# Summing gathered expert rows on TensorE four at a time instead of two, with eleven steps of the second stream placed earlier

## What is computed

```
def _peer(h, w_q, sub_keys, u_tab, v_tab):
    qry = (t @ w_q) ... reshape(n_tok, 8 heads, 2, 128)
    scores = einsum("thpd,hpkd->thpk", qry, sub_keys)
    s_top, i_top = top_k(scores, 16)
    best, pos = top_k(all sums of one of each half, 16)
    idx = take_along_axis(cand_idx, pos)
    gate = softmax(best)
    for each block of 128 tokens:
        u = u_tab[ib]
        act = gelu(einsum("td,thkd->thk", tb, u))
        vv = v_tab[ib]
        out = einsum("thk,thkd->td", gb * act, vv)
```

## Time and profile before

| | |
|---|---|
| median of three runs | 1681.04 us |
| the profiled execution's own time | 1669.39 us |
| its span | 1667.6 us |
| PE busy | 1478.8 us (89%) |
| DVE busy | 1106.1 us (66%) |
| ACT busy | 583.5 us (35%) |
| POOL busy | 824.9 us (49%) |
| bytes moved by DMA | 477.15 MB, of it 268.47 MB by the gathers' queue |
| first gather issued | 313.2 us |
| last gather issued | 1107.4 us |

### The profile page before, as it was taken

One profiled execution on the slowest core, in us unless ns is written; L12 is line 12 of the kernel. 1 busy time (PEld: TensorE's weight loads), 2 busy tenths in 40 slices (PEclk: granted clock), 3 DMA queues, 4 the chain that ended last, 5 costly groups with the idle time before them and its releaser, 6 DMA issues.

```text
span 1667.6 us, 22193 instructions
## 1 busy us (share of the span) xinstructions
PE 1478.8 (89%) x8310; PEld 1059.6 (64%) x8310; DVE 1106.1 (66%) x2162; ACT 583.5 (35%) x847; POOL 824.9 (49%) x746
## 2 busy tenths in 40 slices
PE   8999999766565699999888885889999999999999
PEld 7997675654221266665443441438999896799987
DVE  4865633798488877877756675417886557468864
ACT  6653331211121222221100001127665454466652
POOL 0025230376767765656667777742675113036640
PEclk9999999987977899999799997999999999999999
DMA  7447860598999999999999999994555545635551
GB/s 281 152 151 301 318 253 26 210 389 304 393 407 371 409 401 402 402 403 403 401 401 394 409 396 402 406 396 161 171 187 190 189 182 222 243 111 202 176 191 38
DMA packets 154252, 477.15 MB, mean 286 GB/s; under 512 B 10017, under 2 KB 12321, under 8 KB 150945
## 3 DMA queue, kind: packets, MB, share of 16 engines
q0 software_dynamic: 73728, 268.47, 41.2%
q1 hardware_dynamic: 80416, 207.27, 34.0%
HBM read 474.65 MB, written 1.05 MB: 285 GB/s over the span
## 4 chain that ended last, share of the span: by engine, by line
PE 54%; DMA 13%; DVE 11%; POOL 10%; issue 5%; ACT 2%; DVEq 0%; ACTq 0%; POOLq 0%
PE ps L673 53%; DMA arena<-in_peer_v,cl 11%; POOL arena L2802 8%; DVE arena L1851 2%; PE ps L677 1%; POOL wring L2802 1%; DVE arena L1466 1%; DMA wring<-in_peer_v,cl 1%; DVE arena L1472 1%; DVE wring L1851 1%; DMA wring<-in_peer_u,arena 1%; DVE arena L1469 0%; DVE cvb L1472 0%; DVE arena L1781 0%; ACT arena L2190 0%
## 5 line engine op out<-in xcount | busy, mean ns | idle before, releaser
L673 PE MATMUL ps<-arena,wring 128*128 128x256 f32 (+2 forms) x2360 | 596.0, 488 | 106.0 <-DMA arena<-in_peer_v,cl 101.2
L673 PEld LDWEIGHTS ps<-arena,wring 128*128 128x128 f32 (+1 forms) x2360 | 333.0, 168 | 352.7 <-DMA arena<-in_peer_v,cl 179.7
L1851 DVE CUSTOM_DVE_ANT_0 arena<-arena 128x1024 f32<-128x1024 f32 x214 | 257.6, 1226 | 134.8 <-DMA arena<-in_peer_u,arena 131.9
L2802 POOL DMA_INDIRECT arena<-in_peer_u,arena x214 | 240.0, 1121 | 192.4 <-DVE arena L1809 78.2
L2802 POOL DMA_INDIRECT arena<-in_peer_v,cl x214 | 229.2, 1071 | 77.3 <-issue 60.4
L673 PE MATMUL ps<-hhl,wh 128*128 128x256 f32 (+1 forms) x1056 | 252.4, 323 | 1.2 <-POOL hhl L2812 0.7
L2190 ACT ACT_TABLE_LOAD x64 | 82.1, 1283 | 392.9 <-DVE arena L1851 266.1
L1466 DVE TENSOR_TENSOR wl<-wring,wh 128x2048 fp32r<-128x2048 f32 (+1 forms) x76 | 168.1, 2212 | 60.0 <-ACT wh L2193 58.2
L673 PE MATMUL ps<-hhl,wl 128*128 128x256 f32 x704 | 198.7, 282 | 0.0
L673 PEld LDWEIGHTS ps<-hhl,wh 128*128 128x128 f32 x1056 | 175.8, 190 | 19.5 <-POOL hhl L2812 2.5
L2193 ACT ACTIVATE wh<-wring 128x2048 fp32r<-128x2048 f32 (+1 forms) x78 | 146.1, 1874 | 70.7 <-PE ps L673 68.9
(11 more groups left out here) (257 smaller groups left out, 2025.4 us busy)
## 6 DMA issues: line engine op xcount, KB each, us to landing
wring<-in_ups SPq DMA_DIRECT2D x33, 2048.0 KB, 9.2
wring<-in_ada SPq DMA_DIRECT2D x24, 2048.0 KB, 9.9
wring<-in_ffn_w_down SPq DMA_DIRECT2D x12, 2048.0 KB, 9.0
wring<-in_w_in SPq DMA_DIRECT2D x8, 2048.0 KB, 8.3
wring<-in_ffn_w_down SPq DMA_DIRECT2D x6, 1536.0 KB, 7.6
wring<-in_peer_wq SPq DMA_DIRECT2D x4, 2048.0 KB, 16.1
wring<-in_attn_w_qkv SPq DMA_DIRECT2D x4, 2048.0 KB, 8.4
wring<-in_w_out SPq DMA_DIRECT2D x2, 2048.0 KB, 9.7
```

The lines of the kernel that those rows point to most:

```text
L673: return pe.matmul(o, l, r, start=start, stop=stop)
L1851: ve.tensor_tensor_reduce(out=o, in0=o, in1=h2[:, t, :], scale=1.0, scalar=0.0, op0=MUL, op1=ADD, accum_out=dots[j % 2][:, k:k + 1]).then_ ...
L2802: po.indirect_dma_start(out=ring[n % NR], out_offset=None, in_=table, in_offset=bass.IndirectOffsetOnAxis(ap=which, axis=0)).then_inc(S[f" ...
```

## The change

Two edits. First, PE uses v four rows at a time: at each row with m % 4 == 3 it waits for the four rows one after the other, multiplies each for the first 512 columns, and then all four for the second 512. Second, the first eleven thresholds of `woven` become 2, 5, 7, 10, 12, 15, 17, 20, 22, 25, 27; from the twelfth on they are as before (49, 55, ...). Since `woven` serves PE, ACT and DVE, the second edit moves the steps on all three.

```
--- before.py
+++ after.py
@@ -445,7 +445,7 @@
                 if n == half:
                     next(context, None)
                     half = None
-                elif n >= (4 * (steps + 1) if steps < 11 else 44 + 56 * (steps - 10) // 10):
+                elif n >= (5 * (steps + 1) // 2 if steps < 11 else 44 + 56 * (steps - 10) // 10):
                     steps += 1
                     if next(context, None) == "half":
                         half = n + 3
@@ -1190,9 +1190,9 @@
                     s = what[1]
                     pe.wait_ge(*at("v_w", 2 * s + 2))
                     tr(take(("wT", s), "v_wT", s + 1)[:, 0:128], wt).then_inc(S["p_wT"], 1)
-                elif what[0] == "use" and ROWS[what[1]][0] == "v" and ROWS[what[1]][2] % 2 == 1:
+                elif what[0] == "use" and ROWS[what[1]][0] == "v" and ROWS[what[1]][2] % 4 == 3:
                     _, s, m = ROWS[what[1]]
-                    if m == 1:
+                    if m == 3:
                         pe.wait_ge(*at("v_wT", s + 1))
                         if s == 0:
                             for i in (5, 6):
@@ -1200,7 +1200,7 @@
                         elif s == 4:
                             pe.wait_ge(*at("v_add", 1))
                     for i in range(2):
-                        for k in range(m - 1, m + 1):
+                        for k in range(m - 3, m + 1):
                             n = NTH["v", s, k]
                             q, c = four_of(k)
                             if i == 0:
```

## The result

The changed kernel took **1690.28 us** (median of 20 runs, 1682.91 to 1697.09) where the kernel before took 1681.1 us (20 runs, 1674.81 to 1691.36): a ratio of 1.0049, with a 95% interval of 1.0034 to 1.0065. It is slower by 9.2 us. The forecast was 1679.5 us with a range of 1668 to 1689. The time lies just outside, and near where the rival "the ring runs short" stood (1691).

What follows compares the result with a forecast made beforehand. DMA was taken to bound the gathers, at about 404 GB/s with PE also full from 600 us. Terms -1.0 - 0.5 = -1.5 us took 1669.39 to 1667.9; adding 11.65 gave 1679.5, range 1668 to 1689.

Steps and rivals of the forecast that it cites:

- the ring runs short: Slower rival, 800 to 1060 us: first pair's buffers free about 2.5 us later, 0.4 us lost per group, +10, 1691; chance 0.11.
- part 2: Later release of rows 0 and 1 of a four to POOL's gathers of u: wanted after 15.0 us, available 14.9; taken as 0.
- Part 1: Four rows of v side by side on PE: at best 118 us of PE time, 1.0 us booked on the path.
- the 1.0 us booked at 895.67: The DMA loss from 900 to 920, after POOL waited 3.72 us for PE until 895.67, booked as recovered by fours.
- Part 3: Earlier steps: DVE's 2.09 us wait for head 2's scores goes, won at 335, given back at 402; 0, at most 2.1 us.
- Part 4: SP's context loads, at 417.18, start about 1.7 us sooner and enter a DMA dip: gain 0.5 us, between 0.3 and 0.7.
- Part 5: The tail, PE's last use after the last row lands at 1117.55: finish stays 1.8 us, nothing gained.
- The faster rival: DMA dips at 400 to 420, 510 and 900 fill and DVE's 2.1 us stay: -12, 1669; chance 0.17.
- the dip at 510: DMA window 510 to 520 at low rate, a 3.2 us loss; POOL there stands only for its own issue.
- the 1.99 us: POOL's time for a gather at 510 and 980 beside DVE's arithmetic, where others take 0.94; said to decide those dips.
- The clock rival: Slower: PE, standing more between bursts from 600 us on, falls towards half clock; about +13, 1694; chance 0.04.

Runs made afterwards that it cites:

- the hold: Each gather n also waits for the use of row n - 11, buffers unmoved: kernel before 1.0040, both edits 1.0141, fours alone 1.0146 (slow chip).
- early fours: Fours used at the second row's place (m % 4 == 1): 0.9998 with old thresholds, 0.9991 with new (quick chips); new thresholds 1.0044 on a slow chip.
- Late pairs: Two pairs used one after the other at each fourth row, not joined: 1.0007 with old thresholds, 0.9991 with new, against the kernel before.

## Why the prediction was wrong

**The step that failed is part 2, "Release of the first pair", and in it "I take 0".** The numbers were there: 15.0 us wanted, 14.9 available. The correction that I trusted ("each lands sooner than 9.2, and the slack returns") exists, for on quick chips landing fell from 9.3 to 8.0 us and the ratio was 0.9997 twice. On slow chips it does not carry the fours: they cost 0.39% there alone, 0.49% with the steps, and 1.0% with one gather less of cover. The margin of 0.1 us was also finer than its terms. POOL issued 47 gathers in the 60 us from 920 to 980, one in 1.28 us. With that in place of 1.25 the buffer is wanted after 15.3 us and ready after 14.9. The rival, at a chance of 0.11, had the mechanism that the runs with the hold support. That its price came so near, 10 us against 9.2, is luck: it took 0.4 us from each of 25 groups from 800 to 1060, while the trace has a full 405 GB/s from 800 to 900 and its larger losses in a few windows after 940.

Behind it stands a step that I took as mere arithmetic: the sum was made on an execution of 1669.39 us, and **11.65 us were added as a constant** to reach the median of 1681.04. They were no constant. The trace was of the quick kind and the median of the slow kind. On quick chips the forecast from the trace was nearly right (-1.5 us; measured 0.03% less, some 0.5 us, twice). In an execution of 1669 the ring of 12 suffices even for the fours. Where one of 1681 loses its 12 us is known only from the changed kernel, and there it is in the gathers. The price of a later release had to be asked of the slow kind. That gap, larger than the whole sum, ought to have raised the chance of the ring's rival.

Point by point:
- *Part 1, fours.* Right in size: 16 records in 1.86 us for four rows. Of the 1.0 us booked at 895.67 fours alone show 0.2 (387 GB/s from 900 to 920 on a quick chip, for 383), and their ratio was 1.0008. While DMA is full the saving is worth nothing, as the first half of that part said.
- *Part 2.* See above. "Rows 2 and 3 are released no later" is true and misses that rows 0 and 1 now wait for the landing of row 3.
- *Part 3, steps.* DVE's wait went, as forecast. `turn_rows` 1 was to come at 388.7; on the quick chip, with the steps alone, it came at 389.06, 1.75 us sooner than before:

```profile
389.06 0.47 PE L677 MATMUL ps<-cbase,gt 128*128 128x128 f32 x1 [36.55 <-DVE arena L1809]
```

  In the result's trace it is 0.76 us sooner (390.05): the 2.60 us at line 1840, a wait for transposes pushed behind head 2's scores, which I had not booked, took the rest. That wait is in the traces of the new thresholds on slow chips and not on quick ones. The gain was to be given back at the first use of v, by the scores of head 6 ahead of it. That step was wrong: with pairs the steps kept all of it, 400.95 for 402.72, and 0.9985 is 2.5 us (interval 1.0 to 4.0), near the bound of 2.1 that I named. On quick chips the changed kernel kept it there too (400.34 and 400.96) and lost it later. In the result's trace POOL goes on at 403.97. For the pairs the 0 was too little by that, and for both edits together it was right within what can be told (0.9997).
- *Part 4.* 415.50 for 417.18 is the 1.7 us forecast. In the dip around it 303 GB/s flow, for 338, so that nothing was gained that a run could show.
- *Part 5.* The end of the gathers adds nothing of its own, right.
- *The faster rival.* Not so in the result: 400 to 420 went at 176 and 303 GB/s, not above 380, and at 510 the dip stayed. By the port rule of the Trainium skill ("SBUF — State Buffer", "Who interferes with whom"), PE's relief could not have filled the dip at 510, and the trace agrees as far as that window. That the rule makes the 1.99 us is not shown: at 948.80 us of the kernel before a gather takes POOL 0.94 us beside the same arithmetic of line 1851. No run here took DVE's work away.
- *The clock rival.* From 600 to 780 the granted clock fell below 1.00 in one window only (0.91 at 700 to 720), though PE waited 11.1 us there for 0.2 before:

```profile
PE ps L673 <- DMA arena<-in_peer_v,cl: 4.7, 5, 1.0
PE ps L677 <- DVE arena L1809: 3.6, 1, 3.6
PE ps L673 <- issue: 2.0, 6, 0.6
PE ps L673 <- DMA wring<-in_peer_v,cl: 0.8, 3, 0.3
```

  Up to 900 DMA kept 401 GB/s. At 900 to 920 the clock was 0.68 with PE 13.26 us busy of 20 while DMA moved 408 GB/s, so the lower clock was not what set the end there.

**What stays open.** Why early fours take back two fifths of the loss with the hold and none without it is not settled; that the fourth row's landing binds in both places is argued from the waits, not shown by a run of its own. Late pairs, which would part the later place from the joined release, ran on quick chips only, where nothing was lost. No trace of the kernel before exists on a slow chip, so its own waits there are known only with the hold. What makes a chip slow in thin stretches is open as well. The traces of slow chips carry no landing times, and some of POOL's releasers in them stand as "remote".

## What to carry to other kernels

Grouping uses to save time on an engine that is off the path also groups the release of buffers: count the ring's cover from the landing of the last member of the group, and where wanted and available differ by 0.1 us in 15, price the shortfall instead of taking zero. If the profiled execution is faster than the median by more than the terms of the sum, or than every run of the comparison, ask what the slower executions lack before adding the gap as a constant. Where such a margin decides, compare on more than one chip: this change gave 0.9997 on one kind and 1.0049 on the other. Its steps alone (0.9985, run on a quick chip only) are the part that beat the kernel before.

## What the runs showed of the hardware

- Chips differ in this kernel, as far as one comparison on each can tell: 1668.5 to 1670.0 us on three, 1680.8 to 1683.5 us on two. In the changed kernel 18.3 of the 19.4 us lie between the first gather and the end of the last use of v (1135.44 - 313.50 against 1116.07 - 312.47), most of them outside 600 to 900 us (381 for 404 GB/s from 900 to 1100 us, 401 for 404 from 600 to 900).
- A ring of eleven buffers for twelve costs 1.08% (17 us) on a quick chip, with uses one gather sooner, though gathers then land after 8.1 us in place of 9.3. The cover alone, shortened by one gather, costs 0.40% (6.9 us) on a slow chip.
- Four rows in four 32-column parts take 1.86 us where two rows take 1.84: the parts run side by side, and a group of two leaves half of it unused.
